# Two output buffers for the late columns, and the shifted half of a z column added out of PSUM

## The reference, cut to what matters

```
z_rwkv, z_conv, z_gate = split(a @ w_in)           # 1792, 1024 and 2048 columns
z_rwkv = z_rwkv + (token_shift(z_rwkv) - z_rwkv) * mu
h = u * sigmoid(gate)                              # u, gate = the two halves of z_conv
g_r, g_c = split(sigmoid(z_gate))
```

## Time and profile before

| | us |
|---|---|
| median of three runs | 3401.3 (3399.9 to 3406.7) |
| the profiled execution | 3405.6 |
| its span | 3403.9 |
| busy PE, VectorE, GpSimd, ScalarE in it | 2719.1, 2378.7, 1978.4, 525.0 |

### The profile page before, as it was taken

The page is one execution under the profiler, slowest core; times in us unless marked ns, Lnnn a source line. Parts: engine busy times, 40 slices in busy tenths (PEclk is TensorE's granted clock), DMA queues, the critical chain, the costliest instruction groups (busy, mean ns, idle before and its releaser), DMA issues.

```text
span 3403.9 us, 41995 instructions
## 1 busy us (share of the span) xinstructions
PE 2719.1 (80%) x15556; PEld 1235.5 (36%) x15556; DVE 2378.7 (70%) x6051; ACT 525.0 (15%) x1166; POOL 1978.4 (58%) x2093
## 2 busy tenths in 40 slices
PE   9988985998989888897867687667766777777787
PEld 7877872333323233233323233232323331222111
DVE  5669898886677765777689877987798747665200
ACT  3221321110121101211010101010111001111101
POOL 1013344665656565566677667776767667666663
PEclk9998996998999999998878887798879788888899
DMA  6558998999999999999999999999999999999995
GB/s 212 197 181 301 334 364 286 373 399 380 371 352 385 390 364 362 340 406 390 410 409 403 405 401 409 397 407 405 400 396 408 406 404 410 409 388 406 410 369 235
DMA packets 385725, 1248.57 MB, mean 367 GB/s; under 512 B 40560, under 2 KB 75120, under 8 KB 384752
## 3 DMA queue, kind: packets, MB, share of 16 engines
q0 software_dynamic: 294912, 1073.87, 81.0%
q1 hardware_dynamic: 90608, 172.01, 14.1%
HBM read 1217.80 MB, written 27.92 MB: 366 GB/s over the span
## 4 chain that ended last, share of the span: by engine, by line
PE 34%; DMA 33%; DVE 16%; POOL 10%; issue 5%; ACT 1%; SPq 1%; POOLq 0%; ACTq 0%; DVEq 0%
DMA e_u<-in_u_tab,e_idx 12%; PE e_acc L1273 8%; DMA e_late<-in_u_tab,e_idx 7%; DMA e_v<-in_v_tab,e_idxT 6%; DVE e_u L2178 5%; PE e_pl L1361 5%; POOL e_v L949 4%; PE e_pd L1156 4%; POOL e_u L941 3%; PE e_acc L1318 3%; PE e_pd L1236 3%; PE e_acc L1343 3%; DVE e_late L2178 2%; PE e_pd L976 2%; DMA shifted_projection<-e_side 2%
## 5 line engine op out<-in xcount | busy, mean ns | idle before, releaser
L2178 DVE CUSTOM_DVE_ANT_0 e_u<-e_u,e_c 128x1024 f32<-128x1024 f32 x776 | 943.3, 1216 | 439.8 <-DMA e_u<-in_u_tab,e_idx 424.4
L941 POOL DMA_INDIRECT e_u<-in_u_tab,e_idx x776 | 757.7, 976 | 651.4 <-DVE e_dots L2178 260.2
L1273 PE MATMUL e_acc<-e_v,e_wd 128*32 128x512 f32 x3096 | 900.5, 675 | 284.5 <-DMA e_v<-in_v_tab,e_idxT 260.6
L949 POOL DMA_INDIRECT e_v<-in_v_tab,e_idxT x774 | 732.8, 947 | 434.7 <-PE e_acc L1273 279.2
L2178 DVE CUSTOM_DVE_ANT_0 e_late<-e_late,e_c 128x1024 f32<-128x1024 f32 x248 | 301.1, 1215 | 132.3 <-DMA e_late<-in_u_tab,e_idx 130.5
L1273 PEld LDWEIGHTS e_acc<-e_v,e_wd 128*32 128x32 f32 x3096 | 122.7, 113 | 736.6 <-DMA e_v<-in_v_tab,e_idxT 493.1
L1361 PE MATMUL e_pl<-e_late,e_v 128*128 128x512 f32 x608 | 342.0, 661 | 54.6 <-DVE e_late L1977 13.5
L1273 PE MATMUL e_acc<-e_late,e_wd 128*32 128x512 f32 x832 | 270.8, 712 | 105.0 <-DMA e_late<-in_v_tab,e_idxT 96.1
L941 POOL DMA_INDIRECT e_late<-in_u_tab,e_idx x248 | 240.5, 970 | 189.8 <-DVE e_dots L2178 148.9
L1906 DVE SCALAR_TENSOR_TENSOR e_gbc<-e_hc,e_cw,e_gbc 128x128 f32<-128x128 f32 x960 | 303.7, 343 | 0.5
L949 POOL DMA_INDIRECT e_late<-in_v_tab,e_idxT x208 | 198.2, 953 | 75.2 <-issue 53.1
(11 more groups left out here) (293 smaller groups left out, 3048.2 us busy)
## 6 DMA issues: line engine op xcount, KB each, us to landing
e_u<-in_w_in SPq DMA_DIRECT2D x38, 512.0 KB, 3.8
e_v<-in_w_in SPq DMA_DIRECT2D x38, 512.0 KB, 6.5
e_v<-in_w_in SPq DMA_DIRECT2D x76, 256.0 KB, 6.4
e_u<-in_u_tab,e_idx POOLq DMA_INDIRECT x776, 9.5
e_v<-in_v_tab,e_idxT POOLq DMA_INDIRECT x774, 9.5
e_zb<-in_w_c SPq DMA_DIRECT2D x48, 256.0 KB, 10.5
e_arena<-in_w_r SPq DMA_DIRECT2D x32, 256.0 KB, 19.8
e_zb<-in_w_r SPq DMA_DIRECT2D x32, 256.0 KB, 6.7
```

Source lines behind the costliest of these rows:

```text
L941: pool.indirect_dma_start(out=rows_in[i], out_offset=None, in_=io["u_tab"], in_offset=bass.IndirectOffsetOnAxis(ap=idx[n % 2][:, j:j + 1], ...
L949: pool.indirect_dma_start(out=rows_in[i], out_offset=None, in_=io["v_tab"], in_offset=bass.IndirectOffsetOnAxis(ap=idxT[n % (LAG + 1)][:, ...
L1273: last = pe.matmul(acc[rows, cols], w[:, at_:at_ + 32], rows_in[row][:, cols], start=(step == 0), stop=True, skip_group_check=True)
L2178: dve.tensor_tensor_reduce(rows_in[i], rows_in[i], c[:, :], 1.0, 0.0, ALU.mult, ALU.add, dots[n % 2][:, j:j + 1]).then_inc(s_dot, 1)
```

## The change

The two buffers `l_zs` and `l_zo` become two output buffers `l_out`, used in turn by the columns that are stored, each with its own semaphore for stores that have landed. For a z column ScalarE makes the first place with one activation (bias the carried value, scale 1 - mu) and the rest with a copy scaled by 1 - mu; VectorE then multiplies `pl`, shifted by one, with mu, adds the buffer in place, and only that frees `pl`. ScalarE waits for the store of two outputs before. The sigmoid of a conv gate goes into the buffer that the conv column after it doesn't use, so it waits for the store just before; the conv column itself waits for the store of two before on VectorE. `s_lf` now tells of a finished output, `s_lo` of the scaled copy. Apart from this, `s_second` is gone, and its two counts are taken on `s_brstd` (3 and 4).

```diff
-        l_zs, l_zo = side[:, 0:LATE_T + 1], side[:, LATE_T + 1:2 * LATE_T + 1]
+        l_out = [side[:, i * 513:i * 513 + LATE_T] for i in range(2)]
...
             def late_store(m):
-                if kind(m) == "z":
-                    sp.wait_ge(s_lo, m + 1)
-                else:
-                    sp.wait_ge(s_lf, m + 1)
-                block_store(1, m, l_zo, s_lst)
+                sp.wait_ge(s_lf, m + 1)
+                o = stores_until(m)
+                block_store(1, m, l_out[o % 2], s_lst[o % 2])
...
             def late_out(m):                                  # ScalarE
                 act.wait_ge(s_lu, CHUNKS * (m + 1))
-                i = stores_until(m)
+                o = stores_until(m)
+                out = l_out[o % 2]
...
-                else:
-                    act.wait_ge(s_lst, 16 * i)
+                if kind(m) == "conv gate":
+                    act.wait_ge(s_lst[(o + 1) % 2], 16 * ((o + 1) // 2))
+                    act.activation(l_out[(o + 1) % 2], pl[:, :], ACT.Sigmoid).then_inc(s_lf, 1)
+                elif o >= 2:
+                    act.wait_ge(s_lst[o % 2], 16 * (o // 2))
                 if kind(m) == "z":
-                    act.activation(l_zs[:, 0:1], col(z_last_b, column(m)), ACT.Copy)
-                    act.activation(l_zs[:, 1:], pl[:, :], ACT.Copy, scale=col(vec, COL["mu"] + column(m)))
-                    act.activation(l_zo, pl[:, :], ACT.Copy, scale=col(omm, column(m))).then_inc(s_lf, 1)
-                if kind(m) == "conv gate":
-                    act.activation(l_zs[:, 0:LATE_T], pl[:, :], ACT.Sigmoid).then_inc(s_lf, 1)
+                    act.activation(out[:, 0:1], pl[:, 0:1], ACT.Identity, scale=col(omm, column(m)), bias=col(z_last_b, column(m)))
+                    act.activation(out[:, 1:], pl[:, 1:], ACT.Copy, scale=col(omm, column(m))).then_inc(s_lo, 1)
                 if kind(m) == "gate":
-                    act.activation(l_zo, pl[:, :], ACT.Sigmoid).then_inc(s_lf, 1)
+                    act.activation(out, pl[:, :], ACT.Sigmoid).then_inc(s_lf, 1)
...
             def late_out(m):                                  # VectorE
+                o = stores_until(m)
+                out = l_out[o % 2]
                 if kind(m) == "z":
-                    dve.wait_ge(s_lf, m + 1)
-                    dve.tensor_tensor(l_zo, l_zs[:, 0:LATE_T], l_zo, ALU.add).then_inc(s_lo, 1)
+                    dve.wait_ge(s_lo, m + 1)
+                    dve.scalar_tensor_tensor(out=out[:, 1:], in0=pl[:, 0:LATE_T - 1], scalar=col(vec, COL["mu"] + column(m)),
+                                             in1=out[:, 1:], op0=ALU.mult, op1=ALU.add).then_inc(s_lf, 1)
                 else:
                     dve.wait_ge(s_lu, CHUNKS * (m + 1))
                     dve.wait_ge(s_lf, m)
-                    dve.tensor_tensor(l_zo, pl[:, :], l_zs[:, 0:LATE_T], ALU.mult).then_inc(s_lf, 1)
+                    if o >= 2:
+                        dve.wait_ge(s_lst[o % 2], 16 * (o // 2))
+                    dve.tensor_tensor(out, pl[:, :], l_out[(o + 1) % 2], ALU.mult).then_inc(s_lf, 1)
```

More of the change, by code:

```diff
@@ L542, in trunk @@
         s_bx, s_bsq, s_bsum = sem("b_xT_in"), sem("b_x_squared"), sem("b_squares_summed")
-        s_bdve, s_bvar, s_brstd = sem("b_vector_step"), sem("b_variance_inverted"), sem("b_rstd_ready")
+        s_bdve, s_bvar, s_brstd = sem("b_vector_step"), sem("b_variance_inverted"), sem("b_rstd_ready_then_second_tile_kept")
         s_lw, s_lu = [sem(f"l_w_in{i}") for i in range(CHUNKS)], sem("l_w_chunk_used")
-        s_lf, s_lo, s_lst = sem("l_psum_free"), sem("l_z_ready"), sem("l_output_stored")
+        s_lf, s_lo, s_lst = sem("l_output_ready"), sem("l_z_scaled"), [sem(f"l_output_stored{i}") for i in range(2)]
         s_aw, s_am = [sem(f"a_w_in{i}") for i in range(UW)], sem("a_column_tile_in_psum")
@@ L548, in trunk @@
         s_ao, s_ast = sem("a_output_ready"), [sem(f"a_output_stored{i}") for i in range(2)]
-        s_second = sem("a_second_tile_kept")
         s_zlast = sem("a_last_column_kept")
@@ L614, in stored @@
                 if b == 1:
-                    sp.wait_ge(s_lst, 16 * stores_until(m))
+                    for i in range(2):
+                        sp.wait_ge(s_lst[i], 16 * stores_until(m) // 2)
                 elif b is None and m <= FIRST_GATE:
@@ L687, in tail_loads @@
                     if m == 0:
-                        sp.wait_ge(s_lst, 16 * stores_until(COL_TILES))
+                        for i in range(2):
+                            sp.wait_ge(s_lst[i], 16 * stores_until(COL_TILES) // 2)
                     else:
@@ L1333, in behind_product @@
                     pe.wait_ge(s_bT, KT)
-                    pe.wait_ge(s_second, 2)
+                    pe.wait_ge(s_brstd, 4)
                 if j == 0:
@@ L1553, in second_kept @@
                 act.activation(wd[i][:, 0:KT // 2 * P].rearrange("p (k t) -> p k t", t=P), ahead[:, first:first + KT // 2, P:],
-                               ACT.Copy).then_inc(s_second, 1)
+                               ACT.Copy).then_inc(s_brstd, 1)
             def block_square(k):
```

## The result

The changed kernel took 3379.0 us (median of 5 runs, 3372.9 to 3381.3) beside 3399.9 us (5 runs, 3391.3 to 3406.7) for the kernel before: ratio 0.9937, 95% interval 0.9920 to 0.9955, or 21 us less, between 15 and 27. Run again in another comparison it gave 0.9934 (0.9915 to 0.9954). The forecast of 3393 was 14 us too high, and its range ended at 3381, above what was measured.

What follows compares the result with a forecast made beforehand. Gathers were taken to bound later tiles, PE alone the four-slot late columns. Removed waits -20.0, VectorE's lag +9.7 and weights +2 gave -8.3 us: 3393 against the median of 3401.3, range 3381 to 3404.

Steps and rivals of the forecast that it cites:

- The removed waits: PE's late products waiting for ScalarE, held by late stores, mainly in four-slot columns: 20.0 us of idle taken away.
- The lag of VectorE: Behind z columns PE waits for VectorE, which now reads the bank last: 9.7 us added.
- all lags paid: Every z column's wait for VectorE counted in full, none hidden behind gathers: 14.2 us added instead of 9.7.
- The stretch that I let grow by 4.1: 630 to 750 us, columns 3, 4, 6 and 7: lags of 8.6 us together, taken as 4.1 of growth.
- Weights late next: Four-slot columns, where half-column weight loads become late once the store gap is gone: 2 us added, between 0 and 8.
- Column 8 at nothing: Column 7's late store leaves VectorE idle 5.2 us, but transfers run at 403 GB/s: 0 us taken.
- Identity without a table load: ScalarE's new function at z columns loads no table; the rival, 14 loads of 1.28 us, gave 3411, chance 0.02.
- More is gained: Rival: VectorE's lags hide behind gathers and column 8's 5.2 us counts; -19.6 us, 3382, chance 0.10.
- It cancels: Rival: all VectorE lags are paid and weights cost 2; -4 us, 3397, chance 0.25.
- The lock of PE and VectorE: Rival: each keeps the other late, 2.4 us in all 13 z columns with a follower; +11 us, 3412, chance 0.08.
- waits for ScalarE under 6: Sign: PE's late products wait for ScalarE under 6 us in all instead of 24.7.
- the shrinking short stretches: Sign: 908 to 960 us shrinks by 4 to 5, 1320 to 1368 by 5 to 6, 1368 to 1428 by 5.

Runs made afterwards that it cites:

- experiment 7: The kernel before, one output buffer, with SyncE's store of a late column one slot behind it and ahead of the weight load: 3368.5 us, ratio 0.9904.
- experiment 1: The changed kernel, but ScalarE's copy frees the bank and VectorE works in the output buffer alone, shifted half left out: 3369.6 us, 0.9906 to the kernel before.
- Experiment 6: The kernel before with 17 products by zeros ahead of PE's wait for the bank at seven columns: 3396.6 us, ratio 0.9981.
- experiment 5: The changed kernel with VectorE's late z and conv work ahead of its slot's dot: 3369.3 us, ratio 0.9903 to the kernel before.

## Why the prediction was wrong, step by step

**The removed waits: mis-sized, and the step that failed.** The 20.0 us of idle time were right: in experiment 7, which removes those stalls and adds nothing, the late products wait 19.7 us less for ScalarE, and PE has 21.2 us less idle time in tiles 1 to 3. Their worth was not 20.0 but 32 to 33 (experiments 1 and 7), because PE's busy time fell by 11.1 too. I took busy time as given and only idle time as what a wait costs. The rows were on my page: 0.89 and 0.82 in the column of the granted clock of the two four-slot columns that I used for their 89% and 95% busy, against 1.00 in 630 to 750 us. Part of that busy share was the same work at half speed, so PE was also less close to its bound there than I said. Experiment 6 shows the cause apart from the waits: it shortens none of them, and filling them is worth 6.5 us (2.4 to 10.5). That part of the gap was shown by itself, in the time. That the clock is all of the 12 us between 20 and 32 rests on single profiled executions: the clock share falls by 13.1 in experiment 7 and by 19.6 in experiment 1, and what is left of the busy time is the same in both.

The Trainium skill (TensorE: Matmul & The Clock Gate, "Terms") gives the price of a stretch at the lower clock as its length times one half. In column 12 the stretch at 0.50 was 3.4 us long, which by that rule is 1.7; the rows above have 1.65, so the trace agrees.

**The lag of VectorE: right in size, in part by luck.** I put 9.7 on it. From experiment 1 to the changed kernel there are 8 to 10 us, and 8 to 12 from experiment 5. But it is made up otherwise. PE waits for z adds 18.0 us, where it waits 3.9 for ScalarE in experiment 7: 14.1 more, the 14.2 of "all lags paid". Its whole idle time is only 7 to 9 us above that of experiments 1 and 7, so some of the lag did hide, and the waits behind columns 0, 3, 6 and 13 bring stretches at half clock, which I hadn't priced. The stretch that I let grow by 4.1 grew by 2.3 in one execution and by 0.5 in the other.

**Weights late next: right.** 2 us forecast. PE's late products wait for weights 9.2 us in one wait before, and 11.6 in four after; without the longest, 9.6, three short waits of 2.0 us together are new.

**Column 8 at nothing: right.** VectorE's 5.2 us of idle time before its add are gone, and slots 66 to 84 of tile 1 didn't get shorter: 64.8 us before, 66.3 and 64.9 after. Transfers ran there at 404 GB/s before and 397 after.

**Identity without a table load: right.** L1609 appears 14 times with 351 ns and no load; PE goes on 1.81 us after its last product where VectorE is ready, 1.75 forecast.

**The rivals.** "More is gained" gave 3382, near the measured time, but for reasons that didn't happen: the lags hid only in part and column 8 brought nothing. "It cancels" failed by the missing clock term. The lock of PE and VectorE didn't come: the longest of 13 waits is 3.6 us, 1.4 on average. Of what I said would show it, waits for ScalarE under 6 came (1.1), and so did the shrinking short stretches, by more than I said: by 5.6 us (4 to 5 said), and 7.9 and 7.1 (5 to 6, and 5). The waits for VectorE missed: 24.3 us, counted as the 6.1 before were, against 15 to 20.

With a clock term the sum comes nearer, but not all the way. Behind the store stalls of the kernel before, stretches at 0.50 begin at 606, 927, 958, 1337 and 1425 us, 3.4 to 6.8 us long and 30.6 in all, half of which is 15.3. The changed kernel has three of 3.4 us behind its waits for VectorE instead, at 591, 652 and 724, and the one of 6.8 at 952; half of these is 8.5. The first three no row of before could show. -8.3 - 15.3 + 8.5 = -15.1, against -21 measured. The missing 6 us have no place in the runs: the low stretches that lie behind no store stall also moved, and idle time fell by 12.5 instead of 8.3. The sum of the halves is an upper figure too, as PE isn't busy throughout each stretch (5.5 of 6.8 us at 1337).

## What to carry to other kernels

A stall of TensorE costs its idle time and, when it is followed by a stretch at the lower clock, half of that stretch: look at the granted clock behind each stall before you price it, on both sides of the sum. Before a second buffer is bought against a late store, look at what the store waits behind in its issuing queue: here issuing it a slot earlier and ahead of a weight load was worth 33 us against the change's 21. And work that frees a bank belongs ahead of, not behind, other work of its slot: that order alone was worth the 8 to 12 us that the PSUM add cost.

## What was not expected of the hardware

- PE at 1.2 GHz behind waits of 3.46 and 4.74 us, and behind some as short as 2.06 (kernel before, at 605 us) and 1.84 (kernel after, at 951), but not behind one of 1.88 (kernel before, at 941), nor behind a wait of 3.40 that had 2.3 us of products by zeros ahead of it. In these runs products by zeros kept the clock at 1.00 where it fell without them.
- Four 128x512 products took 1.98 us at 2.4 GHz and up to 3.78 behind a stall (kernel before, at 1338 us).
- The changed kernel's stretches repeat within 1 to 2 us (slots 29 to 66 of tile 1: 111.6 and 110.0), and the places where the clock falls repeat too: behind columns 0, 3 and 13 in both of its executions, behind column 6 in one of them only, where the wait was 1.9 us long instead of 1.2.
